# Two transformer networks on one core: one 512-column matmul for the high and low activations in the feed-forwards and output products

## The reference

```
def _ffn(h, p):
    return (jax.nn.silu(h @ p['w_ff_gate']) * (h @ p['w_ff_up'])) @ p['w_ff_down']
...
x = _post(x, f, gate, g, b)        # layernorm(ALPHA * x + gate * f); the second network: x + f
```

## Time and profile before

| | us |
|---|---|
| three runs | 2903.91, 2900.65, 2901.09 |
| median | 2901.09 |
| span of the profiled execution | 2903.9 |
| PE busy in it | 2702.2 |
| DVE busy in it | 2064.8 |
| ACT busy in it | 1522.6 |

### The profile page before, as it was taken

How to read it: one execution, slowest core, us unless ns; L and a number is a source line. 1 busy time by engine, 2 the same in 40 slices (tenths; PEclk the granted TensorE clock), 3 DMA queues, 4 the chain that set the end, 5 groups by cost and what they waited for, 6 DMA issues and landing times.

```text
span 2903.9 us, 64449 instructions
## 1 busy us (share of the span) xinstructions
PE 2702.2 (93%) x26388; PEld 2563.9 (88%) x26388; DVE 2064.8 (71%) x3683; ACT 1522.6 (52%) x3209; POOL 0.2 (0%) x4
## 2 busy tenths in 40 slices
PE   7988899999989989899989898999999899998998
PEld 5988889999988879799979887798998699996998
DVE  4987878778878787666658798876665665565655
ACT  4555355555665345454565553465545555455554
POOL 0000000000000000000000000000000000000000
PEclk8999999999999999999999899999999899998999
DMA  8453445455554434355425433344654145541554
GB/s 294 150 190 131 137 155 169 139 180 183 167 181 137 140 117 160 127 175 188 146 95 163 148 125 113 103 152 167 190 186 131 59 134 180 187 140 47 165 183 158
DMA packets 120493, 442.20 MB, mean 152 GB/s; under 512 B 13296, under 2 KB 15472, under 8 KB 118816
## 3 DMA queue, kind: packets, MB, share of 16 engines
q1 hardware_dynamic: 108416, 392.86, 41.9%
q10 hardware_dynamic: 11808, 45.42, 4.7%
HBM read 437.18 MB, written 1.05 MB: 151 GB/s over the span
## 4 chain that ended last, share of the span: by engine, by line
PE 67%; DVE 22%; ACT 6%; DMA 3%; issue 2%; SPq 0%; ACTq 0%; DVEq 0%
PE lin L462 17%; PE lin L463 16%; PE lin L464 16%; DVE w_lo L1718 5%; DVE arena L1890 5%; DMA w_raw<-in_stream 2%; ACT w_hi L1104 2%; PE lin L475 1%; PE lin L478 1%; PE lin L479 1%; DMA a_raw<-in_ada 1%; PE aux L580 1%; PE aux L671 1%; PE aux L650 1%; PE lin L493 1%
## 5 line engine op out<-in xcount | busy, mean ns | idle before, releaser
L1718 DVE TENSOR_TENSOR w_lo<-w_raw,w_hi 128x1024 fp32r<-128x1024 f32 x722 | 876.6, 1221 | 329.0 <-ACT w_hi L1104 323.0
L462 PE MATMUL lin<-h_hi,w_hi 128*128 128x256 f32 x3456 | 1000.1, 289 | 6.2 <-DVE h_lo L1826 3.3
L463 PE MATMUL lin<-h_lo,w_hi 128*128 128x256 f32 x3456 | 987.6, 286 | 0.0
L464 PE MATMUL lin<-h_hi,w_lo 128*128 128x256 f32 x3456 | 987.1, 286 | 0.0
L1104 ACT ACTIVATE w_hi<-w_raw 128x512 fp32r<-128x512 f32 x1446 | 828.8, 623 | 297.0 <-DMA w_raw<-in_stream 203.3
L462 PEld LDWEIGHTS lin<-h_hi,w_hi 128*128 128x128 f32 x3456 | 673.8, 195 | 16.6 <-issue 5.9
L463 PEld LDWEIGHTS lin<-h_lo,w_hi 128*128 128x128 f32 x3456 | 673.7, 195 | 0.3
L464 PEld LDWEIGHTS lin<-h_hi,w_lo 128*128 128x128 f32 x3456 | 673.2, 195 | 0.0
L462 PE MATMUL lin<-s_hi,w_hi 128*128 128x256 f32 x1520 | 441.9, 291 | 10.5 <-DVE s_lo L1826 3.6
L463 PE MATMUL lin<-s_lo,w_hi 128*128 128x256 f32 x1520 | 434.5, 286 | 0.8 <-issue 0.8
L464 PE MATMUL lin<-s_hi,w_lo 128*128 128x256 f32 x1520 | 434.2, 286 | 0.0
(11 more groups left out here) (289 smaller groups left out, 3542.9 us busy)
## 6 DMA issues: line engine op xcount, KB each, us to landing
w_raw<-in_stream SPq DMA_DIRECT2D x723, 512.0 KB, 3.6
a_raw<-in_ada ACTq DMA_DIRECT2D x80, 512.0 KB, 3.5
arena<-in_first SPq DMA_DIRECT2D x6, 1024.0 KB, 14.5
X<-in_tokens SPq DMA_DIRECT2D x2, 1024.0 KB, 13.8
s_f<-in_first SPq DMA_DIRECT2D x2, 1024.0 KB, 19.1
arena<-in_const ACTq DMA_DIRECT2D x1, 1856.0 KB, 10.5
arena<-in_small ACTq DMA_DIRECT2D x1, 1536.0 KB, 13.8
out<-arena SPq DMA_DIRECT2D x1, 1024.0 KB, 3.9
```

Of the source, the lines that this page charges most:

```text
L462: used(pe.matmul(o, whi, hi[:, k, :], start=k == 0, stop=False), first)
L463: pe.matmul(o, whi, lo[:, k, :], start=False, stop=False)
L464: mm = pe.matmul(o, wlo, hi[:, k, :], start=False, stop=k == kcs - 1)
L1718: dve.tensor_tensor(w_lo[:, m % SLOTS, :], w_raw[:, m % RAW, :], w_hi[:, m % SLOTS, :].bitcast(F32), ALU.subtract).then_inc(sems["lo_ready ...
```

## The change

In the five feed-forwards and the five output products the high and low activations lie behind one another in one tensor (`h_both`, `s_both`), so that one matmul of 512 columns multiplies w_hi with both. The bank then holds two halves: columns 0 to 255 collect w_hi·x_hi and w_lo·x_hi, columns 256 to 511 collect w_hi·x_lo. ACT moves the second half (`low_half`), DVE adds the first half to it from PSUM (`add_half`) and now counts `lin_evac`. Silu moves behind that addition and becomes an instruction of its own on the buffer. All other products stay as they were, and only their tensors' names change.

```diff
+            def tile_products(o, w, x, start, stop, wide):
+                if wide and stop:
+                    first = pe.matmul(o[:, 0:S], w[:, 1], x[:, 0], start=False, stop=False)
+                    return first, pe.matmul(o[:, 0:2 * S], w[:, 0], x, start=False, stop=True)
+                if wide:
+                    first = pe.matmul(o[:, 0:2 * S], w[:, 0], x, start=start, stop=False)
+                    return first, pe.matmul(o[:, 0:S], w[:, 1], x[:, 0], start=False, stop=False)
...
-                    dense_together(2, ("h_ready", h0))
+                    dense_together(2, ("h_ready", h0), wide=True)
                     for c in range(2, 2 * HALF):
-                        dense(h_hi, h_lo)
+                        dense(h_both, wide=True)
...
-            def arrived(tiles=KC):
+            def arrived(tiles=KC, halved=False):
                 at.tile += tiles
+                if at.halved and not halved:
+                    act.wait_ge(sems["lin_evac"], n.at("lin_evac"))
+                at.halved = halved
...
+            def low_half(dst, tiles=KC, scale=1.0):
+                o = arrived(tiles, True)
+                act.activation(dst, o[:, S:2 * S], ACT.Copy, scale=scale).then_inc(sems["low_half"], 1)
+                split_to(at.tile // TILES + SLOTS)
...
-                        moved(act.activation(gate_buf[:, c % 2, :], o[:, 0:S], ACT.Silu))
-                        o = arrived()
-                        moved(act.activation(y_buf[:, c % 2, :], o[:, 0:S], ACT.Copy))
+                        low_half(g)
+                        act.wait_ge(sems["lin_evac"], n.at("lin_evac"))
+                        act.activation(g, g, ACT.Silu).then_inc(sems["ff_gate"], 1)
+                        low_half(y_buf[:, c % 2, :])
...
+            def add_half(dst, product, scale=None):
+                o = lin[(product - 1) % 4][:, 0:S]
+                dve.wait_ge(sems["low_half"], at.up("low_half"))
+                if scale is None:
+                    dve.tensor_tensor(dst, dst, o, ALU.add).then_inc(sems["lin_evac"], 1)
+                else:
+                    dve.scalar_tensor_tensor(dst, o, scale, dst, ALU.mult, ALU.add).then_inc(sems["lin_evac"], 1)
...
-                        dve.wait_ge(sems["lin_evac"], evac(2))
                         y = y_buf[:, c % 2, :]
+                        up = evac(2)
+                        add_half(gate_buf[:, c % 2, :], up - 1)
+                        add_half(y, up)
+                        dve.wait_ge(sems["lin_evac"], up)
+                        dve.wait_ge(sems["ff_gate"], at.up("ff_gate"))
                         step(dve.tensor_tensor(y, gate_buf[:, c % 2, :], y, ALU.mult))
```

More of the change, by code:

```diff
@@ L453, in done, with dense, dense_together @@
                 tile_at[n.at("lin_done")] = max(at.tile, tile_at.get(n.at("lin_done") - 1, 0))
-            def dense(hi, lo, ready=None, kcs=KC):
-                o = bank()[:, 0:S]
+            def tile_products(o, w, x, start, stop, wide):
[5 more added lines that the diff above has]
+                    return first, pe.matmul(o[:, 0:S], w[:, 1], x[:, 0], start=False, stop=False)
+                first = pe.matmul(o[:, 0:S], w[:, 0], x[:, 0], start=start, stop=False)
+                pe.matmul(o[:, 0:S], w[:, 0], x[:, 1], start=False, stop=False)
+                return first, pe.matmul(o[:, 0:S], w[:, 1], x[:, 0], start=False, stop=stop)
+            def dense(x, ready=None, kcs=KC, wide=False):
+                o = bank()
                 for k in range(kcs):
-                    whi, wlo, first = weight()
+                    w, first = weight()
                     if ready:
                         pe.wait_ge(sems[ready[0]], ready[1] + k + 1)
[L462 to L467, removed]
+                    mm, last = tile_products(o, w, x[:, :, k, :], k == 0, k == kcs - 1, wide)
+                    used(mm, first)
+                done(last)
+            def dense_together(chunks, ready, wide=False):
                 banks, start = [bank() for _ in range(chunks)], at.tile
@@ L473, in dense_together @@
                         at.tile = start + c * KC + k
-                        whi, wlo, first = weight()
-                        mm = pe.matmul(o[:, 0:S], whi, h_hi[:, k, :], start=k == 0, stop=False)
+                        w, first = weight()
+                        mm, last = tile_products(o, w, h_both[:, :, k, :], k == 0, k == KC - 1, wide)
                         used(mm, first if c == 0 else k == KC - 1)
-                        pe.matmul(o[:, 0:S], whi, h_lo[:, k, :], start=False, stop=False)
-                        mm = pe.matmul(o[:, 0:S], wlo, h_hi[:, k, :], start=False, stop=k == KC - 1)
                         if k == KC - 1:
-                            done(mm)
+                            done(last)
             def token_major():
@@ L929, in _ @@
                     for c in range(KC):
-                        dense(s_hi, s_lo, ready if c == 0 else None)
+                        dense(s_both, ready if c == 0 else None)
                     ready = "h_ready", n.at("h_ready")
@@ L1074, in _ @@
                 for c in range(KC):
-                    dense(s_hi, s_lo, ready if c == 0 else None)
+                    dense(s_both, ready if c == 0 else None, wide=True)
                 n.up("r_ready", KC)
@@ L1870, in feed_forward @@
                     dve.wait_ge(sems["r_ready"], at.now("r_ready"))
-                    residual(x, ALPHA if scaled and i == 0 else 1.0, scaled, lambda c: extra(i, "down", c))
+                    for c in range(KC):
+                        down, g = evac(), gate_buf[:, c % 2, :]
+                        add_half(g, down, gate(c) if gate else None)
+                        dve.wait_ge(sems["lin_evac"], down)
+                        dve.scalar_tensor_tensor(x[:, c, :], x[:, c, :], ALPHA if gate and i == 0 else 1.0, g, ALU.mult, ALU.add
+                                                 ).then_inc(sems["r_ready"], 1)
+                        n.up("r_ready")
+                        if gate and c >= 1:
+                            dve.wait_ge(sems["r_ready"], at.now("r_ready"))
+                            summed_up(x, c)
+                        extra(i, "down", c)
                 dve.wait_ge(sems["r_ready"], at.now("r_ready"))
```

113 lines of the change are left out of this document (56 added, 57 removed).

## The result

The changed kernel takes 2921.3 us (median of four runs, 2916.0 to 2928.8), the kernel before 2901.2 in the same job: a ratio of 1.0072 [1.0055, 1.0089], **20 us slower**. The prediction was 2860 us, in a range of 2830 to 2898.

What follows compares the result with a forecast made beforehand. The distance between PE's matmuls was taken as the bound, with little DVE room in the first feed-forward. Later feed-forwards -50.7, output products -4.6 and +1, first feed-forward +9, ends +4: -41.3 us from 2901.1, forecast 2860 us, range 2830 to 2898.

Steps and rivals of the forecast that it cites:

- On that picture the 512-column matmul costs 216 ns (the load behind it is covered): PE, each tile: 216 ns plus 120 for the 256-column matmul, 336 in place of 360, 24 ns less.
- The picture: PE: the next weight load runs beside the current matmul, takes up to 120 ns, and shows only where columns take less.
- 50.7: Gain in us in the second to fifth feed-forward: 2112 tiles at 24 ns each, if DVE and ACT keep up.
- first rival: All float32r matmuls keep 13.3 ns extra: 227 ns for 512 columns, stretches of 183 us, 2885 us in all; chance 0.22.
- its second: A 512-column float32r matmul costs twice a 256-column one: 240 ns, stretches of 190 us, 2918 us in all; chance 0.12.
- The first feed-forward: DVE has no room beside the convolution; additions and waits cost +9 us, ends 0 and +16, stretch about 204 us.
- the additions' price: DVE: an addition of 256 columns from PSUM takes 424 ns, 476 with a scale as well.
- the 1.17 us between the two additions of a round: Up parts: DVE's gate addition, ACT's Silu and move of the up product, then DVE's second addition, 1.17 us start to start.
- DVE's room in the later feed-forwards: DVE's round stays below PE's: 5.04 against 5.38 us in up parts, 3.0 against 3.70 in down parts.
- nothing lost between up and down parts: The last `s_lo` comes about 2.8 us after the product; PE needs it only after ten tiles, 3.36 us.
- The small places: First two output products +1 us (ends -3 and +6), ten stage ends +4, other three output products -4.6.
- both slower cases: 512-column matmul at twice the cost (2918 us, chance 0.12); DVE-ACT round as bound in all up parts (2932 us, chance 0.08).

Runs made afterwards that it cites:

- experiment 5: Kernel before in the new layout, with third feed-forward up-part matmuls of 64 to 512 columns; 256, 320, 384 and 512 took 120, 147, 173 and 227 ns.
- experiment 6: Kernel before, third feed-forward up parts with 256 and 512 columns over weights of 8 to 128 columns; over 8 weight columns 117 and 227 ns.
- experiment 7: 512-column matmul and additions only in the last four feed-forwards, equal matmul sizes grouped within a product: 2887.4 us against 2902.2 for the kernel before, ratio 0.9951.
- experiment 8: Changed kernel with ACT moving the up product's low half before it waits for the gate's addition and does Silu: 2915.0 us, ratio 1.0044.
- experiment 4: Changed kernel's additions kept, but three 256-column matmuls per tile in place of the 512-column form: 2934.3 us, ratio 1.0117 to the kernel before.

## Why the prediction was wrong

**The step that failed: "On that picture the 512-column matmul costs 216 ns (the load behind it is covered)".** It costs 227 in a row of its kind and 236 (most between 233 and 241) in turn with 256 columns, which take 118 then. The picture was that the 13 ns above columns / 2.4 are the rest of the weight load; experiments 5 and 6 show them at four lengths from 256 to 512 columns and, for 512 columns, at every width of the weights (13 to 18). What they come from stays open. By that sum a tile gains 13.3 ns, one fixed part less; 5 of them are lost again where the sizes alternate (experiment 7 gets about 3 back), and the starts of the stretches, some at half clock, take a little more. The four later feed-forwards gained 14.2 us, 6.7 ns a tile, not 50.7. By the prediction's own signs, 236 ns and 187 us lie between its first rival (227 and 183) and its second (240 and 190).

Of the three rows under the picture, were of another form: plain float32 has 216 ns per instruction next to float32r at 227. Those of the earlier trace rows (48 weight columns, 113 to 120 ns) spoke against it, and I read "0.11 to 0.12" as agreement: had the load been the cause, they should have come near 107. Those of the earlier trace rows, half clock with 0.21 us, stand at a floor: 128 and 192 columns take the same 213 ns at half clock. That the extra part is gone at half clock is true all the same, and for 512 columns too: the starts at 615.23 and 615.66 above are 0.43 us apart, which is 512 / 1.2 (427 ns). So more time per weight load was not what made it vanish in the earlier trace rows; a 512-column matmul at full clock has as much, and has the extra part. Why it goes with the clock is not shown.

Plain float32 instructions of experiment 5 stand 216 ns apart, float32r ones 13.3 ns above columns / 2.4. The Trainium skill ("TensorE: Matmul & The Clock Gate", "Back-to-back issue gap") adds 2.5 ns to columns / 2.4, as the gap of a matmul taken by itself: the trace of experiment 5 agrees for the first (512 column steps and 2.7 ns) and not for the second.

**The first feed-forward** was sized too low: +9 (ends 0 and 16), measured +24.5 and 2.6 behind it. The working came to 206 to 208 us and was then lowered to 204, "counting that some handovers are in the overlaps already". Its 195 us hold the sixteen tiles behind the stage as well; with them it is 223 now. DVE's additions cost what was worked out (58 of them in the stretch, 25.1 us; its busy time rose from 151.6 to 173.3), but its idle time did not shrink: 190.1 - 151.6 = 38.5 us before, 41.3 after. The waits of the old round, for high parts and moves, fell from 35.2 us (below, from the trace before) to 19.6 only, and 16.6 came new for the up product's move; experiment 8 shows that a part of it is ACT standing before Silu and delivering late. Half clock on PE, some 6 us by the estimate above, was in no term of the prediction. A wait that is added on both of two engines makes each late for the other; 10 us of it go away with the order of experiment 8.

```profile
574.90:765.00 190.10, 190.10 (x1587) 190.10 (x1586) 151.56 (x263) 105.28 (x208) 0.00 (x0) 1.00 0.58 184
```
```profile
DVE w_lo L1718 <- ACT w_hi L1104: 23.4, 19, 3.5
DVE X L1843 <- ACT gate_buf L1250: 11.8, 8, 2.1
```

**What held:** the additions' price (0.41 to 0.42 us, 0.48 with a scale), the 1.17 us between the two additions of a round (603.17 and 604.34 above), DVE's room in the later feed-forwards, and nothing lost between up and down parts there (no gap on PE). In the first feed-forward these changes cost 6.4 us. **The small places** were sized at about nothing (+1 for two output products, +4 at ends, -4.6 for the others); all else took some 10 us in the profiled pair, and 13 by the median of experiment 4, but hardly any in that one's profiled execution. As kernels without the additions there differ by 16 us outside the feed-forwards, what these places cost is not settled.

**The sum by terms:** later feed-forwards +36.5 against the forecast, first feed-forward +18, the rest about +10: together the 64 us between -41 and the +23 of the profiled pair. The rival of 2918 us comes near the result by luck: it had no gain on PE and +9 in the first stage, two errors that cancel. The first rival (347 ns per tile) had the right size for the matmul by itself, counted 13.3 ns per tile where the kernel got 6.7, and had, like the forecast, too little for the first stage. With its 13.3 ns and the measured +27 in place of its +9 it would have come out at about 2903. The range ended at 2898 since both slower cases had small chances; each of the two terms that failed was one that no row of the kernel before showed as it is, and both failed to the same side.

## What to carry to other kernels

Price an instruction form by rows of that very form: a fixed part per instruction is told from a part per column only by two sizes of the same type, and a witness with one of the suspected causes nearly gone (narrow weights) counts for more than one of another type. Look at the granted clock of a row before you compare it with another. Work added to an engine that has a full stage costs there its whole length and the waits it makes in the other engine's queue; so apply such a change by stage. An instruction that waits for another engine should stand behind everything in its queue that does not need it.

## What the runs showed of the hardware

- Float32r matmuls at full clock: columns / 2.4 + 13.3 ns from start to start for 256, 320, 384 and 512 columns, for weights of 128 columns (448 columns took 207 ns, 7 more); between 113 and 117 ns (256) and 227 and 231 ns (512) for weights of 8 to 96. Two runs of 256 cost the same as 512 contiguous columns.
- Below 256 columns it isn't shorter: 64, 128 and 192 columns took 110 to 114 ns at full clock.
- At half clock (granted 0.50) 128, 192 and 256 columns took 213 ns, 512 columns 427: no extra part above columns / 1.2 for the two larger.
- 512 and 256 columns in turn cost 352 ns for two, 5 more than each in its own row; grouped by size 349.5.
- In the first feed-forward the granted clock stayed at 1.00 in the kernels with at most 1.1 us of gaps on PE and was 0.95 to 0.99 in those with 13 to 20. In experiment 5 it fell to 0.50 with no gap on PE, in the midst of 128-column matmuls that stood behind 64-column ones.
